# Three more modulation kinds summed by VectorE, inside the second chunks of three FFN stages

## The chip, the cores and the metric

One core of one Trainium2 chip runs the whole kernel. The metric is device time in microseconds (us), and the time of a kernel is the median of several runs. Three runs of the kernel before are shown here. All arithmetic is in 32-bit floats.

## The reference, cut to what matters

Two trunk layers are computed for 128 context tokens and 512 latent tokens, side by side (640 tokens, 1024 features). Every layer is FFN, token mixing, FFN, each behind a norm with shift and scale and each with a gate:

```python
mod = (silu(c) @ w_mod[l] + b_mod[l]).reshape(..., 3 * N_SUB, D_MODEL)   # 9 vectors a layer
modulated(j, y) = _rmsnorm(y, g[j]) * (1 + mod[:, :, 3*j+1]) + mod[:, :, 3*j]
x = x + 0.5 * mod[:, :, 2] * _swiglu(modulated(0, x), ffn_w_in[l, 0], ffn_w_out[l, 0])
_swiglu(h, w_in, w_out): g, u = split(h @ w_in); return (silu(g) * u) @ w_out
```

`c` is one vector for the latent tokens and `c_ctx` one for the context tokens. So each of the 18 modulation vectors ("kinds", 9 in each of 2 layers) is a product of two rows of 1024 numbers with a 1024 x 1024 block of `w_mod`.

## The kernel before, in words

**Stages.** FFN 0, the even mixer, FFN 1, FFN 2, the odd mixer, FFN 3; in the code `f` is the number of the FFN. The hidden width of 2816 is worked in 11 "doubles" `d` of 256 columns. Doubles 0 to 3, 4 to 7 and 8 to 10 form chunks 0, 1 and 2. After a chunk's doubles comes its output stretch of 8 units `u`, each 128 output features.

**A double.** From double 1 on, the two halves of the tokens and of the features are combined by a Strassen-like scheme with 7 products ("items" t = 0 to 6) in place of 8. Every product is made of three matmuls (high by high, high by low, low by high part), so an item is 2 column blocks x 4 k-tiles x 3 = 24 matmuls, and a double 168. For its items ScalarE rounds the raw weights to the high part (`item_hi`, L1907), VectorE subtracts to get the low part (`item_lo`, L2482), and VectorE forms four sums of raw weight quadrants in place (`weight_sum`, L2503). The low and high parts lie in a ring of 4 slots, so an item's split can run only when TensorE is done with the item 4 before.

**What stands in VectorE's queue.** `double(f, d)` of the vector block writes the order out by hand, and so do those of ScalarE and TensorE; each engine runs its own list in order. For a double that isn't the last of its chunk it is: `item_lo` 4 and 5, `add_p2` (L2795) of both column blocks s = 0, 1, `item_lo` 6, `item_lo` 0 of the next double, the two "c12" additions (L2832; block s waits for `u2_kept`, a copy by ScalarE at L2120), `weight_sum` 0 of the next double (it waits for both raw halves to have landed), "c22" of block 0 (L2842), the next `item_lo` 1, "c22" of block 1 (L2842), `weight_sum` 1, the next `item_lo` 2, `weight_sum` 2, four multiplications (L2860, L2862), `low_hidden` (L2781), the next `item_lo` 3, `low_hidden`, `weight_sum` 3. In the last double of a chunk the splits of the output weights (`out_lo`, L2488) take the place of those of the next double and there are no sums.

**What TensorE waits for.** Item 6 is added onto the bank that c22 reads, so the part of item 6 for block s waits for c22 of block s of the same double:

```python
def free_part(f, d, t, s):
    n = pairs_before(f, d) + s + 1
    ...
    elif t == 6:
        pe.wait_ge(c22_done, n)
```

**Modulation.** Kinds 0 and 1 come from an opening block. The other 16 are made in two ways while the FFNs run.
- By products: `w_mod` comes in 8 "grains" (one k-tile of all 1024 columns, 512 KB) for a kind, and TensorE multiplies them, 4 grains in a "window" that follows an item (`WINDOWS[f][d, t] = (kind, part)`, `mod_products`, L1200).
- By adding: VectorE runs 16 operations (8 grains x 2 vectors) `acc = grain * c + acc` (`add_grains`; L2575 for the first grain, L2578 for the others), then TensorE sums over the partitions (`acc_sums`, L1210). All 16 run between the updates of x in the output stretch of chunk 0 or 1, and `acc_sums` follows item 1 of the next double.

In both cases `keep_kind` (L2550 to L2557) then turns the result and stores it. Products use four grain buffers, adding uses two of them; the accumulators lie in the other two.

**SyncE** issues every load from one queue, in written order, and waits in it for a buffer to come free: `load_in` (w_in of the next double, raw half 0 after `item_lo` 4, raw half 1 after `item_lo` 6), `load_out`, `load_grain`.

Of the kernel before, what the change touches and what calls it, by code (L numbers as in the profile page):

```python
# [64 lines left out]
def trunk(nc, a, out):  # L65

    with ExitStack() as ctx:
# [753 lines left out]
        def _(sp):  # L821
# [62 lines left out]
            def ffn(f):  # L884

                for d in range(DOUBLES):
# [9 lines left out]
                    if last:  # L896
                        load_out(f, c, 0)
                        load_out(f, c, 1)
                    else:
                        load_in(f, d + 1, 0)  # L900
                        load_in(f, d + 1, 1)
# [2591 lines left out]
```

## Time and profile before

| | us |
|---|---|
| median of 3 runs | 2389.56 |
| lowest and highest run | 2386.39, 2391.74 |
| the profiled execution, its own time | 2391.84 |
| its span (first to last instruction) | 2390.1 |
| TensorE busy | 2339.1 |
| VectorE busy | 1581.4 |
| ScalarE busy | 956.8 |

The profile is of one execution. The span is what its views show; 1.74 us of that execution's time lie around it. Engines: PE is TensorE's matmuls, PEld its weight loads, DVE is VectorE, ACT ScalarE, SP SyncE. Two matmuls that follow each other overlap in the records (a matmul of 320 columns is shown as 0.31 us and the next begins 0.147 us after it), so durations of matmuls are not to be added; starts are to be compared.

### The profile page before, as it was taken

The page shows a single profiled execution, that of the slowest core. Times are in us where ns is not written, and L with a number is a line of the kernel's source. Part 1 is how long each engine was busy: PE and PEld are TensorE (multiplying, and loading weights), DVE is VectorE, ACT ScalarE, POOL GpSimd, SP SyncE. Part 2 cuts the span into 40 slices and gives each one's busy share as a digit, 9 for nine tenths or more (in the row PEclk, how much of TensorE's full clock was granted, in tenths as well). Part 3 has the DMA queues.
Part 4 walks back from the last instruction along what each step waited for, and adds up shares of the span by engine and source line. Part 5 has one row for each costly group of instructions (what it writes and reads, how often), then busy time and mean ns, then how long its engine had stood idle before and what let it go on. Part 6 is the DMA issues. An engine that isn't in the chain of part 4 may idle for free.

```text
span 2390.1 us, 39818 instructions
## 1 busy us (share of the span) xinstructions
PE 2339.1 (98%) x16652; PEld 2262.9 (95%) x16652; DVE 1581.4 (66%) x2414; ACT 956.8 (40%) x1497; POOL 0.2 (0%) x4
## 2 busy tenths in 40 slices
PE   7999999999989999999999999999999999999999
PEld 6999999999769999999999999999999999999998
DVE  5876676657767876777587767676245668467463
ACT  6533423344555423414364143244215255234242
POOL 0000000000000000000000000000000000000000
PEclk9999999999999999999999999999999999999999
DMA  8342545322101242434224344333221012322122
GB/s 293 124 157 94 191 141 176 128 67 71 39 19 54 89 159 92 139 124 142 89 79 170 106 159 159 106 111 99 88 71 45 19 54 71 106 71 89 58 93 71
DMA packets 201421, 251.62 MB, mean 105 GB/s; under 512 B 12994, under 2 KB 178074, under 8 KB 201242
## 3 DMA queue, kind: packets, MB, share of 16 engines
q1 hardware_dynamic: 201242, 249.07, 31.4%
q8 instruction: 132, 2.16, 0.4%
q14 instruction: 47, 0.39, 0.1%
HBM read 245.76 MB, written 3.28 MB: 104 GB/s over the span
## 4 chain that ended last, share of the span: by engine, by line
PE 84%; DVE 7%; issue 3%; ACT 3%; DMA 2%; SPq 0%; DVEq 0%; ACTq 0%
PE banks L1053 72%; DMA w_raw<-ffn_w_in 2%; DVE w_lo L2482 2%; PE banks L1200 1%; ACT w_hi L1907 1%; DVE w_raw L2503 1%; PE banks L1391 1%; PE banks L1393 1%; PE banks L1392 1%; PE banks L1478 1%; PE banks L1490 1%; ACT prob L2284 0%; DVE hid_lo L2781 0%; PE banks L1505 0%; PE banks L1671 0%
## 5 line engine op out<-in xcount | busy, mean ns | idle before, releaser
L1053 PE MATMUL banks<-b_hi,w_hi 128*128 128x320 f32 x2496 | 778.4, 312 | 14.3 <-DVE b_lo L2671 5.8
L1053 PE MATMUL banks<-b_hi,w_lo 128*128 128x320 f32 x2496 | 772.2, 309 | 0.0
L1053 PE MATMUL banks<-b_lo,w_hi 128*128 128x320 f32 x2496 | 772.1, 309 | 0.0
L1053 PEld LDWEIGHTS banks<-b_hi,w_hi 128*128 128x128 f32 x2496 | 469.4, 188 | 33.6 <-issue 23.4
L1907 ACT ACTIVATE w_hi<-w_raw 128x1024 fp32r<-128x1024 f32 x296 | 310.2, 1055 | 417.4 <-PE banks L1053 245.6
L2482 DVE TENSOR_TENSOR w_lo<-w_raw,w_hi 128x1024 fp32r<-128x1024 f32 x296 | 361.7, 1224 | 167.8 <-ACT w_hi L1907 166.1
L1053 PEld LDWEIGHTS banks<-b_lo,w_hi 128*128 128x128 f32 x2496 | 469.6, 188 | 0.0
L1053 PEld LDWEIGHTS banks<-b_hi,w_lo 128*128 128x128 f32 x2496 | 469.4, 188 | 0.0
L1053 PE MATMUL banks<-hid_hi,w_hi 128*128 128x320 f32 x1664 | 397.1, 311 | 3.0 <-DVE hid_lo L2781 1.5
L1053 PE MATMUL banks<-hid_hi,w_lo 128*128 128x320 f32 x1664 | 394.0, 309 | 0.0
L1053 PE MATMUL banks<-hid_lo,w_hi 128*128 128x320 f32 x1664 | 393.9, 309 | 0.0
L1053 PEld LDWEIGHTS banks<-hid_hi,w_hi 128*128 128x128 f32 x1664 | 281.7, 188 | 4.8 <-DVE hid_lo L2781 2.3
L1053 PEld LDWEIGHTS banks<-hid_lo,w_hi 128*128 128x128 f32 x1664 | 282.1, 188 | 0.0
L1053 PEld LDWEIGHTS banks<-hid_hi,w_lo 128*128 128x128 f32 x1664 | 281.9, 188 | 0.0
L2510 DVE SCALAR_TENSOR_TENSOR x<-banks,mod,x 128x128 f32<-128x128 f32 x354 | 135.0, 434 | 220.9 <-PE banks L1053 220.9
L2503 DVE TENSOR_TENSOR w_raw<-w_raw 128x1024 f32<-128x1024 f32 x160 | 195.4, 1221 | 17.1 <-DMA w_raw<-ffn_w_in 11.3
L1913 ACT ACTIVATE w_hi<-w_raw 128x1024 fp32r<-128x1024 f32 (+1 forms) x96 | 93.3, 984 | 236.4 <-PE banks L1053 236.4
L2091 ACT ACTIVATE hid_hi<-work 128x640 fp32r<-128x640 f32 x88 | 64.2, 734 | 159.7 <-DVE work L2862 149.0
L2488 DVE TENSOR_TENSOR w_lo<-w_raw,w_hi 128x1024 fp32r<-128x1024 f32 (+1 forms) x96 | 107.7, 1132 | 9.8 <-ACT w_hi L1913 9.1
L1896 ACT ACTIVATE w_hi<-w_raw 128x2048 fp32r<-128x2048 f32 (+1 forms) x26 | 48.0, 1847 | 103.4 <-PE banks L1053 49.4
L2832 DVE TENSOR_TENSOR work<-work,banks 128x320 f32<-128x320 f32 x80 | 38.0, 485 | 75.1 <-ACT work L2120 75.1
L2465 DVE TENSOR_TENSOR w_lo<-w_raw,w_hi 128x2048 fp32r<-128x2048 f32 (+1 forms) x24 | 52.8, 2202 | 47.1 <-ACT w_hi L1896 47.1
(330 smaller groups left out, 2549.5 us busy)
## 6 DMA issues: line engine op xcount, KB each, us to landing
w_raw<-ffn_w_in SPq DMA_DIRECT2D x176, 512.0 KB, 4.8
mod_grain<-w_mod SPq DMA_DIRECT2D x84, 512.0 KB, 6.0
w_raw<-ffn_w_out SPq DMA_DIRECT2D x64, 512.0 KB, 4.5
last_grain<-w_mod SPq DMA_DIRECT2D x44, 512.0 KB, 6.2
w_raw<-ffn_w_out SPq DMA_DIRECT2D x32, 384.0 KB, 3.7
w_raw<-w_in_odd SPq DMA_DIRECT2D x20, 512.0 KB, 4.7
mod_first<-w_mod SPq DMA_DIRECT2D x3, 2048.0 KB, 15.4
w_raw<-w_in_even SPq DMA_DIRECT2D x12, 512.0 KB, 4.9
```

Of the source, the lines that this page charges most:

```text
L1053: ins = pe.matmul(o, w3[w], v3[v][cols], start=first and i == 0, stop=last and i == 2, skip_group_check=onto_read)
L1200: ins = pe.matmul(bank[MODB][b * MOD_ROWS:(b + 1) * MOD_ROWS, 0:KIND_COLS], wide_c[:, kt, :], by_features(grain[q])[:, b], start=kt == 0, ...
L1896: act.activation(split_view(w_hi, kind, parity(unit)), raw_view(kind, parity(unit)), ACT.Copy).then_inc(hi_ready, 1)
L1907: act.activation(ring_in(w_hi, in_slot(d, t)), operand(d, t), ACT.Copy).then_inc(hi_ready, 1)
L1913: act.activation(ring_out(w_hi, out_slot(c, u), CHUNKS[c]), out_operand(c, u), ACT.Copy).then_inc(hi_ready, 1)
L2091: act.activation(hid_hi[:, k + s, :], work[:, s, 0:2, :].rearrange("p a b -> p (a b)"), ACT.Copy)\
L2465: dve.tensor_tensor(split_view(w_lo, kind, parity(unit)), raw_view(kind, parity(unit)), split_view(w_hi, kind, parity(unit)).bitcast(F32), ...
L2482: dve.tensor_tensor(ring_in(w_lo, q), operand(d, t), ring_in(w_hi, q).bitcast(F32), ALU.subtract).then_inc(lo_ready, 1)
L2488: dve.tensor_tensor(ring_out(w_lo, q, n), out_operand(c, u), ring_out(w_hi, q, n).bitcast(F32), ALU.subtract)\
L2503: dve.tensor_tensor(out_, in0, in1, op).then_inc(sums_done, 1)
L2510: ins = dve.scalar_tensor_tensor(out=xs, in0=bank[banks[hf]][:, in_bank], scalar=mod_col(v, layer, 3 * j + 2, d), in1=xs, op0=ALU.mult, op ...
L2832: dve.tensor_tensor(work[:, s, 1, :], work[:, s, 1, :], role(d, s, "C"), ALU.add).then_inc(c12_done, 1)
```

## The change

Before, six kinds are summed by adding (3, 6, 9, 11, 14, 16) and ten by products. After, nine are summed by adding (3, 4, 5, 9, 10, 11, 13, 14, 15) and seven by products (2, 6, 7, 8, 12, 16, 17). FFNs 0, 1 and 2 each keep two added kinds in the output stretches of chunks 0 and 1 and get a third (4, 10, 14), whose 16 operations are put inside doubles 4 to 7 (2, 4, 4 and 6 of them), at five slots of VectorE's list. Its `acc_sums` follows item 6 of double 7, its `keep_kind` the last `out_lo` of that double, and its grains are loaded between those of the weights. The windows move: FFN 0 loses the four of doubles 5 and 6; FFN 1 loses (5, 1) and (6, 1) and gets (2, 4) and (3, 4); FFN 2 loses (2, 1), (3, 1), (5, 1), (6, 1) and gets (9, 4) and (10, 4). The first two grains of an outer kind are now issued behind the first two loads of the output weights.

```diff
-        WINDOWS = ({(1, 4): (2, 0), (2, 4): (2, 1), (5, 1): (4, 0), (5, 4): (4, 1), (6, 1): (5, 0), (6, 4): (5, 1),
-                    (9, 1): (7, 0), (9, 4): (7, 1), (10, 1): (8, 0), (10, 4): (8, 1)},
-                   {(5, 1): (10, 0), (6, 1): (10, 1), (9, 1): (12, 0), (10, 1): (12, 1)},
-                   {(2, 1): (13, 0), (3, 1): (13, 1), (5, 1): (15, 0), (6, 1): (15, 1), (9, 1): (17, 0), (10, 1): (17, 1)}, {})
-        ADDED = ({0: 3, 1: 6}, {0: 9, 1: 11}, {0: 14, 1: 16}, {})
-        SUMS_AT = (4, 1), (8, 1)
+        WINDOWS = ({(1, 4): (2, 0), (2, 4): (2, 1), (9, 1): (6, 0), (9, 4): (6, 1), (10, 1): (7, 0), (10, 4): (7, 1)},
+                   {(2, 4): (8, 0), (3, 4): (8, 1), (9, 1): (12, 0), (10, 1): (12, 1)},
+                   {(9, 1): (16, 0), (9, 4): (16, 1), (10, 1): (17, 0), (10, 4): (17, 1)}, {})
+        ADDED_OUT = ({0: 3, 1: 5}, {0: 9, 1: 11}, {0: 13, 1: 15}, {})
+        ADDED_IN = ({1: 4}, {1: 10}, {1: 14}, {})
+        SUMS = [{**{(doubles_until(c), 1): kind for c, kind in ADDED_OUT[f].items()},
+                 **{(doubles_until(c) - 1, ITEMS - 1): kind for c, kind in ADDED_IN[f].items()}} for f in range(4)]
         ADD_OPS = (3, 3, 3, 3, 2, 1, 0, 1)
+        DOUBLE_OPS = {1: (2, 4, 4, 6)}
+        SLOT_OPS = {2: (0, 0, 0, 2, 0), 4: (0, 0, 1, 2, 1), 6: (1, 1, 1, 2, 1)}
         HALF_KIND = KT // 2
-        FIRST_WINDOW = ((1, 4), None, (2, 1), None)
+        FIRST_WINDOW = ((1, 4), (2, 4), None, None)
...
@@ SyncE, ffn(f), in double d
+                    inner, outer = ADDED_IN[f].get(c), ADDED_OUT[f].get(c) if last else None
+                    done = ops_before(f, d)
+                    ready = done + DOUBLE_OPS[c][d - CHUNK_PARTS * c] if inner is not None else None
+                    if last:
+                        load_out(f, c, 0)
+                    else:
+                        load_in(f, d + 1, 0)
+                    if inner is not None and done // 2 + 2 < (ready + 1) // 2:
+                        load_grain(inner, done // 2 + 2)
+                    if last:
+                        load_out(f, c, 1)
+                    else:
+                        load_in(f, d + 1, 1)
+                        if inner is not None:
+                            for kt in range(max(done // 2 + 2, (ready + 1) // 2), min(ready // 2 + 2, KT)):
+                                load_grain(inner, kt)
+                    if outer is not None:
                         if c == 0 and FIRST_WINDOW[f] is None:
                             rows_free(f)
-                        load_grain(added, 0)
-                        load_grain(added, 1)
...
@@ VectorE, double(f, d)
+                def add_slot(i):
+
+                    if c in ADDED_IN[f]:
+                        slots = SLOT_OPS[DOUBLE_OPS[c][d - CHUNK_PARTS * c]]
+                        add_grains(ADDED_IN[f][c], ops_before(f, d) + sum(slots[:i]), slots[i])
+
                 item_lo(f, d, 4)
+                add_slot(0)
                 if d == 1:
                     form_low(f, 5, quadrants(f)[2][:, :, :])
                 item_lo(f, d, 5)
+                add_slot(1)
                 if d == 1:
                     form_low(f, 6, quadrants(f)[1][:, :, :])
                 for s in range(2):
                     add_p2(f, d, s)
+                    if s == 0:
+                        add_slot(2)
                 item_lo(f, d, 6)
                 if not last and d > 1:
                     item_lo(f, d + 1, 0)
+                add_slot(3)
                 for s in range(2):
+                    if s == 1:
+                        add_slot(4)
                     dve.wait_ge(u2_kept, done + s + 1)
                     dve.tensor_tensor(work[:, s, 1, :], work[:, s, 1, :], role(d, s, "C"), ALU.add).then_inc(c12_done, 1)
...
-                if kind_done is not None:
+                if kind_done is not None and kind_done not in ADDED_IN[f].values():
                     keep_kind(kind_done)
...
                     out_lo(f, c, 3)
+                    if c in ADDED_IN[f]:
+                        keep_kind(kind_done)
```

## Rows read from the trace of the kernel before

**Rows 1.** The page: busy time of each engine.

```profile
PE 2339.1 (98%) x16652; PEld 2262.9 (95%) x16652; DVE 1581.4 (66%) x2414; ACT 956.8 (40%) x1497; POOL 0.2 (0%) x4
```

**Rows 2.** Windows: length; busy us (records) by engine; clock, DMA share, GB/s.

```profile
2130.91:2155.55 24.64, 24.64 (x170) 24.64 (x169) 18.76 (x24) 11.89 (x17) 0.00 (x0) 1.00 0.27 87
1392.77:1419.47 26.70, 26.70 (x202) 25.58 (x201) 19.98 (x30) 12.01 (x17) 0.00 (x0) 1.00 0.45 158
913.18:939.01 25.83, 25.83 (x186) 25.05 (x185) 15.50 (x19) 10.97 (x15) 0.00 (x0) 1.00 0.46 164
```

**Rows 3.** VectorE, FFN 3, double 5: start, length, what, idle before.

```profile
2142.77 1.23 DVE L2482 TENSOR_TENSOR w_lo<-w_raw,w_hi 128x1024 fp32r<-128x1024 f32 x1 [0.59 <-ACT w_hi L1907]
2146.35 1.23 DVE L2482 TENSOR_TENSOR w_lo<-w_raw,w_hi 128x1024 fp32r<-128x1024 f32 x1 [2.35 <-ACT w_hi L1907]
2147.49 0.48 DVE L2832 TENSOR_TENSOR work<-work,banks 128x320 f32<-128x320 f32 x1
2149.18 0.49 DVE L2832 TENSOR_TENSOR work<-work,banks 128x320 f32<-128x320 f32 x1 [1.21 <-ACT work L2120]
2149.59 1.22 DVE L2503 TENSOR_TENSOR w_raw<-w_raw 128x1024 f32<-128x1024 f32 x1
...
2153.07 0.48 DVE L2842 TENSOR_TENSOR work<-work,banks 128x320 f32<-128x320 f32 x1
```

**Rows 4.** FFN 3, double 6: VectorE and the matmul that waits.

```profile
2175.15 1.23 DVE L2503 TENSOR_TENSOR w_raw<-w_raw 128x1024 f32<-128x1024 f32 x1 [0.83 <-DMA w_raw<-ffn_w_in]
...
2178.64 0.48 DVE L2842 TENSOR_TENSOR work<-work,banks 128x320 f32<-128x320 f32 x1
...
2179.18 0.41 PE L1053 MATMUL banks<-b_hi,w_hi 128*128 128x320 f32 x1 [0.26 <-DVE work L2842]
```

**Rows 5.** Windows: FFN 3 doubles 6 and 9, FFN 1 double 5.

```profile
2155.55:2181.03 25.48, 25.14 (x170) 24.64 (x169) 18.76 (x24) 11.88 (x17) 0.00 (x0) 1.00 0.26 83
2286.63:2312.52 25.89, 25.14 (x170) 24.64 (x169) 18.77 (x24) 11.89 (x17) 0.00 (x0) 1.00 0.26 82
939.01:967.11 28.10, 27.21 (x203) 25.59 (x201) 19.98 (x30) 12.00 (x17) 0.00 (x0) 1.00 0.44 150
```

**Rows 6.** VectorE before weight_sum 0: FFN 3 double 9, FFN 1 double 5.

```profile
961.22 1.23 DVE L2503 TENSOR_TENSOR w_raw<-w_raw 128x1024 f32<-128x1024 f32 x1 [1.39 <-DMA w_raw<-ffn_w_in]
...
2306.63 1.23 DVE L2503 TENSOR_TENSOR w_raw<-w_raw 128x1024 f32<-128x1024 f32 x1 [1.24 <-DMA w_raw<-ffn_w_in]
```

**Rows 7.** VectorE, FFN 0, output stretch.

```profile
313.94 1.41 DVE L2575 TENSOR_SCALAR mod_grain<-mod_grain,wide_c 128x1024 f32<-128x1024 f32 x2
315.27 1.28 DVE L2578 SCALAR_TENSOR_TENSOR mod_grain<-last_grain,wide_c,mod_grain 128x1024 f32<-128x1024 f32 x1
316.46 1.13 DVE L2510 SCALAR_TENSOR_TENSOR x<-banks,mod,x 128x128 f32<-128x128 f32 x3
```

**Rows 8.** VectorE, FFN 0, double 4.

```profile
220.22 0.49 DVE L2832 TENSOR_TENSOR work<-work,banks 128x320 f32<-128x320 f32 x1 [1.22 <-ACT work L2120]
```

**Rows 9.** VectorE, FFN 3, double 7, the last of its chunk.

```profile
2188.75 1.23 DVE L2482 TENSOR_TENSOR w_lo<-w_raw,w_hi 128x1024 fp32r<-128x1024 f32 x1 [0.38 <-ACT w_hi L1907]
...
2199.30 0.49 DVE L2832 TENSOR_TENSOR work<-work,banks 128x320 f32<-128x320 f32 x1 [1.27 <-ACT work L2120]
2200.25 1.23 DVE L2488 TENSOR_TENSOR w_lo<-w_raw,w_hi 128x1024 fp32r<-128x1024 f32 x1 [0.46 <-ACT w_hi L1913]
2201.39 0.48 DVE L2842 TENSOR_TENSOR work<-work,banks 128x320 f32<-128x320 f32 x1
```

**Rows 10.** Grains into buffers 0 to 2, FFN 1's first output stretch.

```profile
DMA to landing us min/median/max: 3.4/3.4/6.9
```

**Rows 11.** Windows: double 2 of FFNs 1, 2 and 3.

```profile
803.99:832.22 28.23, 25.82 (x170) 24.63 (x169) 21.87 (x27) 13.55 (x19) 0.00 (x0) 1.00 0.35 113
1255.50:1283.92 28.42, 27.64 (x203) 25.57 (x201) 22.21 (x27) 13.66 (x19) 0.00 (x0) 1.00 0.54 197
1997.45:2025.31 27.86, 25.71 (x170) 24.64 (x169) 21.81 (x26) 13.57 (x19) 0.00 (x0) 1.00 0.26 77
```

More of the change, by code:

```diff
@@ L610, in trunk, with kinds_before, ops_before @@
         ffn_tables(3)
-        WINDOWS = ({(1, 4): (2, 0), (2, 4): (2, 1), (5, 1): (4, 0), (5, 4): (4, 1), (6, 1): (5, 0), (6, 4): (5, 1),
[3 rows of a table removed]
-        ADDED = ({0: 3, 1: 6}, {0: 9, 1: 11}, {0: 14, 1: 16}, {})
-        SUMS_AT = (4, 1), (8, 1)
+        WINDOWS = ({(1, 4): (2, 0), (2, 4): (2, 1), (9, 1): (6, 0), (9, 4): (6, 1), (10, 1): (7, 0), (10, 4): (7, 1)},
[5 more added lines that the diff above has]
+                 **{(doubles_until(c) - 1, ITEMS - 1): kind for c, kind in ADDED_IN[f].items()}} for f in range(4)]
         ADD_OPS = (3, 3, 3, 3, 2, 1, 0, 1)
+        DOUBLE_OPS = {1: (2, 4, 4, 6)}
+        SLOT_OPS = {2: (0, 0, 0, 2, 0), 4: (0, 0, 1, 2, 1), 6: (1, 1, 1, 2, 1)}
         HALF_KIND = KT // 2
-        FIRST_WINDOW = ((1, 4), None, (2, 1), None)
-        BY_ADDING = [kind for f in range(4) for kind in ADDED[f].values()]
-        BY_PRODUCTS = [kind for kind in range(FIRST_KIND, DEPTH * 3 * N_SUB) if kind not in BY_ADDING]
+        FIRST_WINDOW = ((1, 4), (2, 4), None, None)
+        KIND_ORDER = tuple(range(2, DEPTH * 3 * N_SUB))
+        BY_PRODUCTS = (2, 6, 7, 8, 12, 16, 17)
+        BY_ADDING = [kind for kind in KIND_ORDER if kind not in BY_PRODUCTS]
+        def kinds_before(kind):
+            return KIND_ORDER[:KIND_ORDER.index(kind)]
         def products_before(kind):
-            return KT * sum(k < kind for k in BY_PRODUCTS)
+            return KT * sum(k in BY_PRODUCTS for k in kinds_before(kind))
         def adds_before(kind):
-            return 2 * KT * sum(k < kind for k in BY_ADDING)
+            return 2 * KT * sum(k in BY_ADDING for k in kinds_before(kind))
         def added_before(kind):
-            return sum(k < kind for k in BY_ADDING)
+            return sum(k in BY_ADDING for k in kinds_before(kind))
+        def ops_before(f, d):
+            c = chunk_of(d)
+            return sum(DOUBLE_OPS[c][:d - CHUNK_PARTS * c]) if c in ADDED_IN[f] else 0
         def grain_buf(kind, kt):
@@ L642, in trunk @@
         buf_loads, buf_user = [0] * GRAIN_BUFS, [None] * GRAIN_BUFS
-        for kind in range(FIRST_KIND, DEPTH * 3 * N_SUB):
+        for kind in KIND_ORDER:
             for kt in range(KT):
@@ L660, in added_at @@
         def added_at(f, d, t):
-            return ADDED[f].get(SUMS_AT.index((d, t))) if (d, t) in SUMS_AT else None
+            return SUMS[f].get((d, t))
         def kind_done_at(f, d):
@@ L889, in ffn @@
                         load_window(f, where)
-                    added = ADDED[f].get(c) if last else None
-                    if added is not None:
+                    inner, outer = ADDED_IN[f].get(c), ADDED_OUT[f].get(c) if last else None
[15 more added lines that the diff above has]
+                    if outer is not None:
                         if c == 0 and FIRST_WINDOW[f] is None:
                             rows_free(f)
-                        load_grain(added, 0)
-                        load_grain(added, 1)
[L896 to L901, printed above, removed]
+                        load_grain(outer, 0)
+                        load_grain(outer, 1)
                     if last:
@@ L904, in ffn @@
                         load_out(f, c, 3)
-                    if added is not None:
+                    if outer is not None:
                         for kt in range(2, 5):
-                            load_grain(added, kt)
+                            load_grain(outer, kt)
                     if last and d + 1 < DOUBLES:
                         load_in(f, d + 1, 0)
-                    if added is not None:
+                    if outer is not None:
                         for kt in range(5, KT):
-                            load_grain(added, kt)
+                            load_grain(outer, kt)
                     if last and d + 1 < DOUBLES:
                         load_in(f, d + 1, 1)
+                        if c + 1 in ADDED_IN[f]:
+                            load_grain(ADDED_IN[f][c + 1], 0)
+                            load_grain(ADDED_IN[f][c + 1], 1)
                     if d + 1 < DOUBLES:
@@ L1181, in bank_free @@
             def bank_free(f, kind):
[L1183 removed]
+                if kind == KIND_ORDER[0]:
                     pe.wait_ge(first_prod, 2 * f + 2)
                 else:
[L1186 removed]
+                    pe.wait_ge(kind_kept, len(kinds_before(kind)))
             def by_features(tile):
@@ L2898, in ffn @@
                     tail = final and after[0] is not None
-                    added = ADDED[f].get(c)
+                    added = ADDED_OUT[f].get(c)
                     if added is not None:
```

2 lines of the change are left out of this document (removed).

## The prediction, on record before the changed kernel was run

> **What bounds the kernel now.** I read the page first. TensorE is busy for 2339.1 of 2390.1 us and VectorE for 1581.4, two thirds [rows 1]. The average makes VectorE look free, so the question is where in a double the free time lies. The view of windows gives the price of TensorE's own work: a double without modulation takes 24.64 us and has no idle time (busy 24.64), one with a window takes 26.70 us, one with an `acc_sums` 25.83 us [rows 2]. So a window costs 2.06 us, an `acc_sums` 1.19 us, and TensorE alone sets the pace there.
>
> Then I read VectorE's timeline of such a double [rows 3]. It is busy for 18.76 of 24.64 us. From the start of the double (2130.91 us), `item_lo` 6 runs at +11.86, then 2.35 us pass idle until the next `item_lo` 0 at +15.44, which waits for ScalarE, as that waits for a ring slot. The c12 additions follow at +16.58 and +18.27, with 1.21 us idle between them, since block 1 waits for ScalarE's copy. `weight_sum` 0 starts at +18.68 and c22 of block 1 at +22.16. Behind c12 nothing is idle but short waits on ScalarE for results of VectorE itself.
>
> c22 has hardly any room. In double 6 of FFN 3 `weight_sum` 0 waited 0.83 us for a weight load, c22 of block 1 ended at 2178.64 + 0.48 = 2179.12, and TensorE's next matmul, idle for 0.26 us, started at 2179.18 with "DVE work L2842" as what ended its wait [rows 4]. That double took 25.48 us, 0.84 more than 24.64. Two others took 25.89 against 24.64 and 28.10 against 26.70, so 1.25 and 1.40 us were lost [rows 5], and there the same wait was 1.24 and 1.39 us [rows 6]. A delay of `weight_sum` 0 is lost one for one. Exactly: it started at +18.68 in double 5 of FFN 3, at +19.60 in double 6 and at +20.00 in double 9, 0.92 and 1.32 us late for 0.84 and 1.25 us lost; the room is 0.08 us.
>
> **The change, part by part.**
>
> *TensorE's work.* Product kinds go from ten to seven, that is 20 to 14 windows: 6 x 2.06 = 12.36 us saved. `acc_sums` go from six to nine: 3 x 1.19 = 3.57 us added. Balance: -8.79 us.
>
> *The operations added to VectorE.* The first grain's take (315.27 - 313.94) / 2 = 0.67 us each, the others 316.46 - 315.27 = 1.19 us from start to start [rows 7]. 6 and 42 of them make 54 us in twelve doubles.
>
> *Double 4 (two short ones, slot 3).* They stand in front of c12: 1.33 us. The idle time between the two c12 additions is 1.22 us in this double too [rows 8], and is now used up, since ScalarE's copy for block 1 is ready by then. c12 of block 1 is late by about 0.03 to 0.11 us, within the room. Loss 0.
>
> *Doubles 5 and 6 (four each; slots 2, 3, 3, 4).* The one in slot 2 delays `item_lo` 6 by 0.6 us (1.19 less the 0.59 it waited) and with it the load of raw half 1; the 2.35 us idle behind it swallow the rest. Two stand in slot 3, behind the next `item_lo` 0, so the 2.35 us are no cover for them: c12 of block 0 starts at 2147.49 + 2.38 = 2149.87. Then 0.40 for it, and the slot 4 operation, 1.19, sits in front of c12 of block 1, which starts at 2151.46 instead of 2149.18 [rows 3]: 2.28 us late. `weight_sum` 0 and both c22 follow 2.28 us late, and TensorE loses 2.28 - 0.08 = 2.20 us. The weight load has more slack than before, so lateness of a load as in [rows 6] no longer adds. TensorE's stall moves the next double's start by the same amount, and `item_lo` 0 hangs on TensorE, so the delay starts anew in each double and doesn't pile up: 2 x 3 x 2.20 = 13.2 us. Bounds: 0, if idle time that I don't see covers them, and 3 x 1.19 = 3.57 us per double, if none does; 0 to 21.4 us in all. I take the worked value, as [rows 4 to 6] show this very path.
>
> On the price of one such operation the Trainium skill says, in VectorE: DVE Perf Modes, section Mode 1× (REGULAR) — the baseline, that an operation with two tensor inputs in 32 bits gives one result a cycle, and the page's clock is 0.96 GHz; that is an estimate of 1.07 us for 1024 elements, against 1.19 us in the row [rows 7]. By the page each of these doubles would lose 3 x 0.12 = 0.36 us less and the sum would be 2.2 us lower; the row is this very instruction, and the sum goes by it.
>
> *Double 7 (six; slots 1, 1, 1, 2, 1), the last of the chunk.* I walk FFN 3's double 7, with 1.14 us from start to start for a split and 0.40 for a small addition [rows 3, 9]. `item_lo` 4 at 2188.75; an operation, `item_lo` 5, an operation: to 2193.41; `add_p2`, operation, `add_p2`, `item_lo` 6, an operation: to 2197.73. The next one needs grain 7. Its load is issued only when the operation that ended at about 2193.5 is done, behind half of the output weights. Grains landed 3.4 to 6.9 us after issue, median 3.4 [rows 10]; with another load just ahead I take 4.5, so 2198.0. Then this operation, c12 of block 0, the last operation, and c12 of block 1 starts at 2200.8 instead of 2199.30, `out_lo` 0 at 2201.2 instead of 2200.25 (it waited 0.46 us on ScalarE before, so that part is covered), and c22 is 0.95 us late. c22 of block 0 ended at 2201.87 [rows 9] and TensorE was due at 2181.03 + 21.12 = 2202.15 (six of seven items); less 0.15 for the signal that is 0.13 of room: 0.8 us lost. With no wait for the grain it is 0.5, with 6.9 us it is 3.2. Three FFNs: 2.4 us, bounds 1.5 and 9.6, and 0 if c22 isn't what counts.
>
> *What is behind the chunk.* `keep_kind` (some 2 us) now stands behind `out_lo` 3 and ahead of the first x update. VectorE, some 5 us late there, has TensorE's next unit (7 us) before that update is asked for: 0. The outer kind's first grains are issued by the middle of double 7, over 10 us ahead of their use: 0. `acc_sums` behind item 6 finds its sums done.
>
> *Windows moved.* Double 2 of an FFN has stalls of its own: 28.23 us in FFN 1 and 27.86 in FFN 3 without a window, 28.42 in FFN 2 with one [rows 11]. So FFN 2's window there cost only 0.37 us, and taking it away gives 0.37 and not 2.06: +1.69. FFN 1 gets one behind item 4 of double 2, where it can hide those stalls that come later: between 0 and the 1.69 of FFN 2; I take -1.1. FFN 1's double 5 loses its window and the grain loads that delayed its weights, so the 1.40 us lost there go: -1.40 (its new stall is in the 13.2).
>
> **Sum.** -12.36 + 3.57 + 13.2 + 2.4 + 1.7 - 1.1 - 1.4 = +6.0 us on the profiled execution's 2391.84, or 2397.8. That execution is 2.28 above the median 2389.56; taken from the median: 2395.6 us.
>
> **Rivals.**
>
> *A. The operations fit into VectorE's idle time (faster).* The place is c12 to c22 in doubles 5 and 6. For it: the two waits of a double, 2.35 + 1.21 = 3.56 us, are just what three operations need (3.57). If what `item_lo` 0 waits for weren't tied to TensorE's pace, or if TensorE had more room at item 6 than 0.08 us, the whole 13.2 + 2.4 = 15.6 us of stalls would be gone: 6.0 - 15.6 = -9.6, so 2380.0. It decides from c22 of block 1 being done before +22.7. Against it: the order of the slots, and three doubles that lost what they were late. 10 in 100.
>
> *B. Grain 7 is late.* It lands 6 to 7 us after issue as the slowest in [rows 10]; double 7 then loses 2.3 to 3.2 and not 0.8: 4.5 to 7 us more, 2400 to 2402.5. For it: its load has no lead. Against: most single grains land in 3.4. 14 in 100.
>
> *C. The stalls are there but the small terms go the other way.* The stalls of FFN 2's double 2 don't return (1.7 less), and double 7 costs nothing (2.4 less): +1.9, 2391.5, no difference that can be measured. 19 in 100.
>
> **How the numbers follow.** The forecast has 57 in 100. What a measurement here can tell from no change is about 0.2%, 4.8 us, so slower means above 2394.3. My forecast is only 1.3 above that; with its own spread of some 2 us I give 43 of the 57 to slower and 14 to the same. Slower 43 + 14 (B) = 57, same 14 + 19 (C) = 33, faster 10 (A). The range 2388.5 to 2401.5 holds the forecast, C and most of B, and leaves out A and the far end of B.
>
> **What would show it.** Right: in the changed profile doubles 5 and 6 of FFNs 0, 1 and 2 take 26.8 us, with TensorE waiting for "DVE work L2842" (the line moves) by some 2 us; double 4 takes 25.83; double 7 takes 25.4 up to item 7 plus 1.19; c12 of block 0 starts 2.4 us behind the end of the next `item_lo` 0. FFN 0 is faster by some 2 us, FFNs 1 and 2 slower by 4 each. Wrong: doubles 5 and 6 at 24.64 (A); VectorE waiting over 2 us for `mod_grain` or `last_grain` in double 7 (B); a stall growing from double 5 to 6, or waits on `w_lo` in doubles 5 to 7, would show that the delays pile up, which I exclude.

## The result: slower by 13.7 us, the direction as forecast, the size more than twice as large

The changed kernel takes 2403.24 us, the median of five runs (2402.27 to 2405.49). The kernel before takes 2389.56, five runs too (2386.39 to 2391.74). The ratio is 1.0058, with a 95% interval of 1.0047 to 1.0069. The forecast was +6.0 us, 2395.6, with a range up to 2401.5; the measured +13.7 lies beyond that range. The profiled executions differ by 2403.24 - 2391.84 = 11.4 us and their spans by 11.3, which is what the traces can account for. The 2.3 us that are left are the distance of the profiled run of before from its own median.

The page after, its first line and the line of `items`' matmuls (columns as in [rows 1]; behind the bar busy time, mean ns, idle time just before and what ended most of it):

```profile
PE 2334.1 (97%) x16508; PEld 2260.9 (94%) x16508; DVE 1633.4 (68%) x2462; ACT 956.6 (40%) x1497; POOL 0.2 (0%) x4
...
L1078 PE MATMUL banks<-b_hi,w_hi 128*128 128x320 f32 x2496 | 779.6, 312 | 30.6 <-DVE work L2880 18.2
```

Against [rows 1] VectorE has 52 us more to do, close to the 54 of the forecast. TensorE is busy 5.0 us less, and these matmuls now wait 18.2 us for c22 (L2842 before is L2880 now); in the same group of the kernel before it was 2.7.

The windows of doubles 4 to 7 of FFNs 0, 1 and 2 in the changed kernel, four rows for each FFN, answer to [rows 2, 5] (length; busy us of PE, PEld, DVE, ACT and POOL with their numbers of records; granted clock, DMA share, GB/s):

```profile
200.70:226.53 25.83, 25.83 (x186) 25.05 (x185) 16.71 (x21) 10.97 (x15) 0.00 (x0) 1.00 0.36 117
226.53:254.63 28.10, 25.15 (x170) 24.65 (x169) 24.43 (x34) 11.89 (x17) 0.00 (x0) 1.00 0.37 113
254.63:281.78 27.15, 25.14 (x170) 24.64 (x169) 23.36 (x28) 11.88 (x17) 0.00 (x0) 1.00 0.38 116
281.78:308.12 26.34, 25.97 (x187) 24.96 (x185) 24.24 (x32) 11.68 (x17) 0.00 (x0) 1.00 0.48 158
916.33:942.17 25.84, 25.84 (x187) 25.06 (x186) 16.72 (x21) 10.96 (x15) 0.00 (x0) 1.00 0.37 119
942.17:971.42 29.25, 26.22 (x171) 25.99 (x169) 25.15 (x35) 11.77 (x17) 0.00 (x0) 0.94 0.35 109
971.42:998.26 26.84, 25.14 (x171) 24.64 (x169) 22.71 (x27) 12.00 (x17) 0.00 (x0) 1.00 0.39 118
998.26:1025.43 27.17, 25.98 (x187) 24.97 (x185) 24.24 (x32) 11.67 (x17) 0.00 (x0) 1.00 0.50 161
1371.62:1397.45 25.83, 25.83 (x186) 25.05 (x185) 16.71 (x21) 10.97 (x15) 0.00 (x0) 1.00 0.37 117
1397.45:1425.45 28.00, 25.14 (x171) 24.65 (x169) 24.43 (x34) 11.88 (x17) 0.00 (x0) 1.00 0.37 113
1425.45:1454.65 29.20, 26.51 (x170) 26.05 (x169) 24.35 (x29) 11.77 (x17) 0.00 (x0) 0.94 0.35 108
1454.65:1480.39 25.74, 25.74 (x187) 24.96 (x185) 23.32 (x31) 11.67 (x17) 0.00 (x0) 1.00 0.47 155
```

Double 4 loses nothing (25.83). FFN 0 is 0.5 us faster than before from double 1 to double 10, FFNs 1 and 2 are 6.5 and 6.7 us slower, where the forecast had 2 faster and 4 slower each. FFN 1's double 6 is 26.84 - 24.64 = 2.20 us above the plain double, exactly the stall worked out. The other five are not: doubles 5 have 3.46, 4.61 and 3.36 us, doubles 6 of FFNs 0 and 2 have 2.51 and 4.56. The six stalls come to 20.7 us and not 13.2. These 7.5 us are what the prediction lacks, and the experiments are about them. Two of the rows have a granted clock of 0.94, where all those of [rows 2, 5] have 1.00.

*Where double 5 loses more.* VectorE's timeline in the changed kernel, FFN 0, from the end of double 4 (start, length, what, idle time before; double 5 starts at 226.53):

```profile
229.68 0.31 DVE L2575 STREAM_TRANSPOSE mod_turn<-banks 128x128 f32<-128x128 f32 x1
...
231.36 0.83 DVE L2806 TENSOR_TENSOR hid_lo<-work,hid_hi 128x640 fp32r<-128x640 f32 x1 [0.21 <-ACT hid_hi L2116]
...
235.57 1.23 DVE L2507 TENSOR_TENSOR w_lo<-w_raw,w_hi 128x1024 fp32r<-128x1024 f32 x1 [0.38 <-ACT w_hi L1932]
...
243.22 1.22 DVE L2507 TENSOR_TENSOR w_lo<-w_raw,w_hi 128x1024 fp32r<-128x1024 f32 x1 [1.71 <-ACT w_hi L1932]
244.37 1.28 DVE L2603 SCALAR_TENSOR_TENSOR mod_grain<-last_grain,wide_c,mod_grain 128x1024 f32<-128x1024 f32 x1
...
246.76 0.48 DVE L2870 TENSOR_TENSOR work<-work,banks 128x320 f32<-128x320 f32 x1
```

The outer kind's `keep_kind` (six small operations, 229.68 to 231.14) stands ahead of `low_hidden`, so `item_lo` 4 starts at 235.57, +9.04. In the kernel before, in double 5 of FFN 3, which starts at 2130.91, it is at +7.65:

```profile
2138.56 1.23 DVE L2482 TENSOR_TENSOR w_lo<-w_raw,w_hi 128x1024 fp32r<-128x1024 f32 x1 [0.38 <-ACT w_hi L1907]
```

The next `item_lo` 0 starts at +16.69 and not at +15.44, that is 1.25 us late. From there on all is as forecast: c12 of block 0 (246.76) starts 2.39 us behind the place right after `item_lo` 0 (244.37), where the first of the two operations now stands. ScalarE's timeline names the link between the two:

```profile
242.13 1.06 ACT L1932 ACTIVATE w_hi<-w_raw 128x1024 fp32r<-128x1024 f32 x1 [3.77 <-DMA w_raw<-ffn_w_in]
```

ScalarE waits for raw half 0, which is loaded once `item_lo` 4 has freed it: that operation ends at 236.80, SyncE issues the load at 236.82, and it has landed at 242.12. Late operation, late issue, late landing.

### The profile page after: what moved, and what is told of

The parts are those of the page before. It is cut to its first block, busy times and chain, and to the rows that moved or that the text cites. A ratio compares the mean times of both kernels' runs of the same rounds, so it can differ in the third digit from the quotient of the medians.

```text
span 2401.4 us, 39602 instructions
## 1 busy us (share of the span) xinstructions
PE 2334.1 (97%) x16508; PEld 2260.9 (94%) x16508; DVE 1633.4 (68%) x2462; ACT 956.6 (40%) x1497; POOL 0.2 (0%) x4
## 4 chain that ended last, share of the span: by engine, by line
PE 79%; DVE 10%; issue 4%; ACT 4%; DMA 3%; SPq 0%; DVEq 0%; ACTq 0%
PE banks L1078 67%; DMA w_raw<-ffn_w_in 2%; DVE w_lo L2507 2%; ACT w_hi L1932 2%; DVE w_raw L2528 1%; DVE mod_grain L2603 1%; PE banks L1225 1%; PE banks L1416 1%; PE banks L1418 1%; PE banks L1417 1%; PE banks L1503 1%; PE banks L1515 1%; DVE hid_lo L2806 1%; ACT prob L2309 0%; PE banks L1530 0%
## 5 line engine op out<-in xcount | busy, mean ns | idle before, releaser
L1078 PE MATMUL banks<-b_hi,w_hi 128*128 128x320 f32 x2496 | 779.6, 312 | 30.6 <-DVE work L2880 18.2
L2603 DVE SCALAR_TENSOR_TENSOR mod_grain<-last_grain,wide_c,mod_grain 128x1024 f32<-128x1024 f32 x72 | 91.1, 1279 | 0.9 <-DMA last_grain<-w_mod 0.9
```

Source lines behind the costliest of these rows:

```text
L1078: ins = pe.matmul(o, w3[w], v3[v][cols], start=first and i == 0, stop=last and i == 2, skip_group_check=onto_read)
L2603: ins = dve.scalar_tensor_tensor(out=acc, in0=grain[q], scalar=c_of, in1=acc, op0=ALU.mult, op1=ALU.add)
```

## The experiments

Eleven kernels ran, in three groups, each group with its own runs of the kernel before: medians 2391.13 (24 runs), 2390.26 (18) and 2390.25 (17). Ratios are to these.

**e1_order.** The changed kernel with slot 3 ahead of the next `item_lo` 0.

```diff
+                add_slot(3)
                 if not last and d > 1:
                     item_lo(f, d + 1, 0)
-                add_slot(3)
```

> Theory P (place): TensorE's loss in doubles 5 and 6 comes from the two operations that stand behind the next item_lo 0, in front of c12 and c22. Here they stand ahead of it, in the 2.35 us that VectorE waits there; everything else is as in the changed kernel. P: double 6 loses 0.3 to 0.4 us instead of 2.2 to 4.6, double 5 about 1.1 (its weight load of half 0 is late) instead of 3.4 to 4.6, TensorE's clock doesn't fall, and the kernel takes 2385 to 2390 us instead of 2403.2. Rival L (load): what counts is how much work VectorE has in a double, and the order of two neighbours is indifferent: 2402 to 2404, doubles 5 and 6 as before.

Measured: 2392.23 us (11 runs), ratio 1.0004 [0.9995, 1.0013], 11 us below the changed kernel. The stalls of doubles 5 fell to 1.7, 2.2 and 1.7 us and those of doubles 6 to 0.4, 0.5 and 1.1. So the place of two operations behind `item_lo` 0 is worth most of the stall, as the prediction's timeline had it: the 2.35 us of idle time ahead of `item_lo` 0 [rows 3] are a cover only for what stands ahead of it. It missed the expected 2385 to 2390 by some 2 us, in doubles 5. Against the kernel before it is no difference that can be measured.

**e2_short.** The operations of the inner kinds on 8 of 1024 columns (this leaves most of these kinds' sums out), loads and waits as they are.

```diff
+                    n_cols = 8 if kind in (4, 10, 14) else GRAIN
-                    acc, c_of = mod_acc[:, v, :], wide_c[:, kt, v:v + 1]
+                    acc, c_of = mod_acc[:, v, 0:n_cols], wide_c[:, kt, v:v + 1]
```

> Leaves out: the 16 operations inside doubles 4 to 7 work on 8 of 1024 columns, so kinds 4, 10 and 14 are not summed. Number, order, signals and DMAs are those of the changed kernel. Both P and L: the operations' length is gone (some 0.1 us each), doubles 5 and 6 lose at most 0.5 us each, double 7 nothing, and what is left is the change in TensorE's own work and in the early doubles: 2379 to 2382 us. Rival G (grains): the loads of the grains between those of the weights, or the number of instructions and signals, make the weights late; then doubles 5 and 6 still lose over 1 us each and the kernel takes over 2388.

Measured: 2383.75 us (8 runs), ratio 0.997 [0.996, 0.998], 1.75 us above the expected range. Double 7 costs 1.09 us in all three FFNs, nothing beyond its `acc_sums`, so grains and their loads have no price of their own there. But doubles 5 still lose 0.6, 0.9 and 0.7 us and doubles 6 of FFNs 0 and 2 lose 0.5 and 1.0, with almost no work added. The time of the operations is not the cause of that.

**e4_both.** All the work, spread 5, 3, 3, 5, slot 3 ahead as in e1_order, and the outer kind kept at the opening of double 4.

```diff
-        DOUBLE_OPS = {1: (2, 4, 4, 6)}
-        SLOT_OPS = {2: (0, 0, 0, 2, 0), 4: (0, 0, 1, 2, 1), 6: (1, 1, 1, 2, 1)}
+        DOUBLE_OPS = {1: (5, 3, 3, 5)}
+        SLOT_OPS = {0: (0, 2, 0, 2, 1), 1: (0, 0, 0, 2, 1), 2: (0, 0, 0, 2, 1), 3: (1, 1, 1, 1, 1)}
```

> All 48 operations are there, but each stands where VectorE waits: 5, 3, 3, 5 of them in doubles 4 to 7, always two ahead of the next item_lo 0 and one between the two c12; acc_sums of the outer kind follows item 0 and its keep_kind opens doubles 4 and 8, so that double 5 doesn't start late. P: no double of the three second chunks loses more than 0.5 us but for a late weight load (up to 1.3 us, one or two of them), and the kernel takes 2379 to 2384 us, faster than both. L: VectorE has the same work, so 2400 or more.

Measured: 2387.56 us (11 runs), ratio 0.9983 [0.9974, 0.9992]. Faster than both kernels, and some 4 us above what was expected. Doubles 5 lose 0.4, 0.2 and 0, but doubles 4 lose 1.2, 0.5 and 0.3 and doubles 6 of FFNs 0 and 2 1.9 and 1.5. In the three that lose over 1 us a weight load lands late.

**e5_probe.** The kernel before with scratch operations in FFN 3, which feed nothing. It ran once, as did e7_probe, and both are read by the lengths of FFN 3's doubles alone.

```diff
+                ahead, behind, between = PROBES.get((f, d), (0, 0, 0))
                 item_lo(f, d, 6)
+                probe(ahead)
                 if not last and d > 1:
                     item_lo(f, d + 1, 0)
+                probe(behind)
                 for s in range(2):
+                    if s == 1:
+                        probe(between)
                     dve.wait_ge(u2_kept, done + s + 1)
```

> The kernel before with operations added in FFN 3 alone, which has no modulation (a scratch result of the same form, 128 x 1024, 1.19 us each; 9 of them). Double 5: two behind the next item_lo 0 and one between the c12, as in the change. Double 6: two ahead of the next item_lo 0 and one between. Double 9: three behind and one between. P: double 5 takes 24.64 + 2.20 = 26.8 us, double 6 24.7 to 25.0 (24.64, the small excess, and up to 0.8 if its load is late), double 9 28.1 (four times 1.19, less 1.21 and 0.08 = 3.47), and if a stall of 3.4 us lowers TensorE's clock, up to 1.7 more. L: doubles 5 and 6 lose the same.

Windows of FFN 3's doubles 5 and 9 in e5_probe:

```profile
2130.97:2157.81 26.84, 25.13 (x171) 24.64 (x169) 22.17 (x27) 11.88 (x17) 0.00 (x0) 1.00 0.25 80
2288.05:2317.33 29.28, 26.53 (x170) 26.04 (x169) 24.39 (x29) 11.88 (x17) 0.00 (x0) 0.94 0.23 72
```

Two behind `item_lo` 0 and one between cost 26.84 - 24.64 = 2.20 us to the hundredth; two ahead and one between cost nothing (double 6: 24.64). Three behind and one between cost 29.28 - 24.64 = 4.64, where one operation more than in double 5 gives 2.20 + 1.19 = 3.39 (the 3.47 of the expectation is 0.08 too much). The row has the reason, a clock of 0.94.

**e3_keep.** The changed kernel with `acc_sums` of the outer kind one item earlier and its `keep_kind` at the opening of doubles 4 and 8. Nothing else moves.

```diff
-        SUMS = [{**{(doubles_until(c), 1): kind for c, kind in ADDED_OUT[f].items()},
+        SUMS = [{**{(doubles_until(c), 0): kind for c, kind in ADDED_OUT[f].items()},
...
+                outer_done = SUMS[f].get((d, 0))
+                if outer_done is not None:
+                    keep_kind(outer_done)
                 item_lo(f, d, 4)
```

> The changed kernel with all its operations in their slots (2, 4, 4, 6), and one thing moved: the outer kind's acc_sums stands one item earlier and its keep_kind opens doubles 4 and 8 instead of closing them. Theory K (keep_kind at the end of double 4 delays item_lo 4 of double 5 by 1.4 us, and by it the load of raw half 0 and the next item_lo 0): the stall of double 5 falls from 3.45, 4.61 and 3.35 us in FFNs 0, 1, 2 to the 2.20 that the prediction had, the granted clock no longer falls in FFN 1's double 5, double 6 keeps its 2.2 to 2.5, and the median is 3.5 to 4.5 us below the changed kernel's 2403.2: 2399 to 2400. Rival J (the load of half 0 is late by the lateness of transfers alone): double 5 keeps 3.3 us or more in at least two FFNs, 2402 to 2404. Rival S (the keep_kind's 1.4 us is only moved): double 4 loses what double 5 gains, 2402 to 2404.

Measured: 2400.51 us (5 runs), ratio 1.0036 [1.0023, 1.0048]. Windows of doubles 5 and 6 of FFNs 0, 1, 2:

```profile
226.22:253.06 26.84, 25.14 (x171) 24.64 (x169) 23.30 (x28) 11.88 (x17) 0.00 (x0) 1.00 0.38 118
253.06:280.89 27.83, 25.13 (x170) 24.63 (x169) 23.36 (x28) 11.77 (x17) 0.00 (x0) 1.00 0.37 114
...
941.31:968.15 26.84, 25.14 (x171) 24.64 (x169) 23.30 (x28) 11.88 (x17) 0.00 (x0) 1.00 0.38 119
968.15:994.99 26.84, 25.14 (x170) 24.64 (x169) 23.36 (x28) 11.88 (x17) 0.00 (x0) 1.00 0.38 118
...
1393.85:1420.70 26.85, 25.14 (x170) 24.65 (x169) 23.32 (x28) 11.88 (x17) 0.00 (x0) 1.00 0.38 118
1420.70:1449.20 28.50, 25.14 (x171) 24.64 (x169) 23.36 (x28) 11.76 (x17) 0.00 (x0) 1.00 0.36 111
```

All three doubles 5 lose exactly 2.20 us now, and double 4 nothing: theory K holds in its mechanism and in the size of the stall. The median is 2.7 us below the changed kernel's and not 3.5 to 4.5, because doubles 6 of FFNs 0 and 2 came to 3.2 and 3.9 us.

**e6_order_keep.** e1_order and e3_keep together.

> Both of the moves together, operations 2, 4, 4, 6: slot 3 stands ahead of the next item_lo 0 (as in e1_order) and keep_kind opens double 4 (as in e3_keep). If the two causes are separate (place of slot 3; late start of double 5), the gains add: e1_order's 2392.2 falls by 1.2 to 1.5 us for each of three doubles 5 (its stalls there of 1.7, 2.2 and 1.7 us become 0.4 to 0.6), 2387.5 to 2389. If the order alone had hidden the late start already, it stays at 2392. TensorE's granted clock stays at full in all FFN doubles.

Measured: 2387.26 us (11 runs), ratio 0.9983 [0.9974, 0.9992]. The gains add: doubles 5 lose 0.4, 0.7 and 0.8 us. Doubles 6 keep 0.5, 0.7 and 1.6.

**e8_split.** The same with another split.

```diff
+        DOUBLE_OPS = {1: (4, 3, 3, 6)}
+        SLOT_OPS = {0: (0, 1, 0, 2, 1), 1: (0, 0, 0, 2, 1), 2: (0, 0, 0, 2, 1), 3: (1, 1, 1, 2, 1)}
```

> Both moves and another split, 4, 3, 3, 6 operations in doubles 4 to 7, so that doubles 5 and 6 hold just the three that the two waits (2.35 + 1.21 us) cover, two ahead of the next item_lo 0 and one between the c12 additions. Theory P: doubles 5 and 6 lose 0 to 0.4 us each except where a transfer is late, double 4 loses 0 to 0.5, double 7 0.5 to 1.5; total of stalls about 5 us against 20.7 + 2 in the changed kernel: 2385 to 2387.5. Rival L (transfers that become later as VectorE's work moves toward its loads): as e4_both, one or two doubles of each FFN lose 1.5 us more, 2387.5 to 2389.

Measured: 2386.05 us (8 runs, 2382.64 to 2389.86), ratio 0.9981 [0.997, 0.9992]. Doubles 4 lose nothing, doubles 5 nothing, doubles 6 0.2, 0 and 0.7. It is 4 us faster than the kernel before. Its runs overlap with those of e4_both, e6_order_keep and e11_split_fetch, so that it is the best of the four is not shown.

**e7_probe.** e5_probe's operations placed anew.

```diff
-            PROBES, probes = {(3, 5): (0, 2, 1), (3, 6): (2, 0, 1), (3, 9): (0, 3, 1)}, [0]
+            PROBES, probes = {(3, 5): (0, 3, 1), (3, 6): (0, 2, 1), (3, 9): (0, 2, 1)}, [0]
```

> The kernel before with scratch multiply-adds in FFN 3 alone (on x, into the free sums' buffer; their results are used by nothing). Double 5: three behind the next item_lo 0 and one between the c12 additions, so a stall of 3.39 us if the delay is lost one for one; double 6: two behind and one between, 2.20 us; double 9: the same two and one, where the kernel before lost 1.25 us to a late load. Theory C (a stall of about 3 us or more of TensorE is followed by a stretch at the lower granted clock, and one of 2.2 is not): double 5 takes 24.64 + 3.39 + 0.8 to 1.1 = 28.8 to 29.1 us with a granted clock of 0.5 for 3.4 us behind the stall; double 6 takes 26.84 at full clock. Rival: the clock falls by chance, not by the stall: double 5 takes 28.03 at full clock. Double 9: 26.84 if the late load and the operations hide one another (the longer counts), 28.1 if they add.

Windows of FFN 3's doubles 5, 6 and 9, and of the stretch behind double 5's stall:

```profile
2132.49:2161.51 29.02, 26.38 (x170) 26.15 (x169) 24.25 (x29) 11.88 (x17) 0.00 (x0) 0.94 0.24 74
2161.51:2188.35 26.84, 25.14 (x170) 24.64 (x169) 21.46 (x26) 11.99 (x17) 0.00 (x0) 1.00 0.26 79
2293.95:2320.79 26.84, 25.14 (x170) 24.64 (x169) 22.18 (x27) 11.88 (x17) 0.00 (x0) 1.00 0.26 79
2153.00:2161.00 8.00, 5.36 (x27) 5.13 (x26) 7.17 (x10) 3.26 (x4) 0.00 (x0) 0.79 0.01 2
```

Double 5 lost 29.02 - 24.64 = 4.38 us: 3.39 by the operations and 1.0 by the clock. Double 9 lost 2.20 and not 2.20 + 1.25, but it doesn't test what it was built for: its half 1 landed at +18.59 and not at +19.91 as in the kernel before, so no load was late. Double 6 tests it. Its half 1 landed at +19.57 (+19.50 in the kernel before, where it cost 0.84 us), `weight_sum` 0 started at +20.96 behind the operations without waiting for it, and the double lost 2.20. So a late half 1 and operations on VectorE hide one another, and the longer counts.

**What makes half 0 late in double 6.** In the queues of FFN 2's double 6, from the issue of half 0 (1434.4) to its landing (1441.0), the changed kernel has one packet that FFN 1's double 6 (979.4 to 984.8) has not. The queues in FFN 2 (queue and kind: packets, MB, share of 16 engines):

```profile
q1 hardware_dynamic: 1195, 1.19, 58.2%
q8 instruction: 1, 0.02, 0.9%
```

In FFN 1 the view has the first line alone (1056 packets). The two transfers of half 0 from issue to landing, FFN 2 and then FFN 1:

```profile
DMA to landing us min/median/max: 4.4/5.3/6.2
...
DMA to landing us min/median/max: 3.9/4.4/4.9
```

These packets are 16 KB each. The changed kernel has 131 of them, one for 256 of its 33,544 recorded instructions on TensorE (matmuls, weight loads and their sequencer's), some 18.4 us apart; that they carry TensorE's program is inferred from this count. Over the changed kernel and nine of its variants there are 80 loads of half 0 in doubles 5 and 6. In 17 such a packet starts between the issue of the first transfer and a microsecond before the landing of the second, and the second takes 5.2 to 6.9 us. In the other 63 it takes 4.7 to 5.1. The two groups don't overlap. In FFN 2's double 6 a packet lay there in all ten kernels, so for this double there is no load without one to compare.

**e9_fetch.** The changed kernel with the same satisfied wait repeated on TensorE near the start, which shifts where the packets fall.

```diff
-            pe.wait_ge(rows_in, 16 * 7)
+            for _ in range(58):
+                pe.wait_ge(rows_in, 16 * 7)
```

> The changed kernel with 58 waits more on TensorE near the start (the same wait on rows_in, long satisfied, in front of the transposes of small_rows, where TensorE has idle time soon behind). Nothing else is changed. The traces so far show one DMA packet of kind 'instruction' (16 KB, queue 8) for about every 256 instructions of TensorE, some 18.4 us apart. Theory F (such a packet, when it falls between a weight load's issue and its landing, makes the load land 0.4 to 2 us later): the packets move about 4 us earlier, so that of FFN 2's double 6 (at +12.25 us, half 0 landed at +15.6 instead of +14.2) and of FFN 0's (at +9.55, landed at +14.6) leave the load's stretch; double 6 of FFN 2 loses 2.2 us instead of 4.6, FFN 0's 2.2 instead of 2.5, and double 7 of FFN 1 (packet at +10.8, landed at +16.2) 0.5 instead of 1.4; nothing in doubles 5: 3.6 us less, 2399 to 2400.5. Rival (lateness is of the address or by chance): the landings of half 0 in FFN 2's double 6 stay at +15.6 to +16.1 as in all six kernels with the change's windows so far, 2402.5 to 2404.

The trace shows 29 instructions more on TensorE and not 58, and the packets of the two doubles moved by 2.1 and 2.4 us and not by 4: in FFN 0's double 6 from +9.55 to +7.43 and in FFN 2's from +12.25 to +9.84. FFN 0's left its load's stretch, half 0 landed at +14.1 and the double lost 2.20. FFN 2's stayed in it, nearer its start; half 0 landed at +14.7 instead of +15.6 and the double lost 2.6 instead of 4.6, 1.1 of which is the clock, which stayed at full here. The median is 2401.59 (2398.39 to 2404.92, 5 runs), above the expected 2399 to 2400.5, and its runs overlap with those of the changed kernel: at this length of kernel the median doesn't tell it, the traces do.

**e10_keep_fetch.** e3_keep and e9_fetch together, every operation in the changed kernel's slots.

> e3_keep (keep_kind opens double 4) and the 58 waits of e9_fetch. If the three causes (start of double 5, instruction packets beside the loads, clock) are all that the prediction lacked, every one of the six doubles 5 and 6 loses the 2.20 us that it worked out, where no packet falls into a half 0 load, and the median is what it forecast, 2395 to 2397 (e3_keep: 2400.5, less 1.0 for FFN 0's double 6, 1.7 for FFN 2's, 0.9 for FFN 1's double 7). If something else holds the doubles, 2399 to 2401.

Measured: 2396.03 us (7 runs, 2395.04 to 2397.5), ratio 1.0026 [1.0015, 1.0036]. Windows of the six doubles 5 and 6:

```profile
226.30:253.17 26.87, 25.13 (x171) 24.64 (x170) 23.30 (x28) 11.88 (x17) 0.00 (x0) 1.00 0.39 118
253.17:280.00 26.83, 25.13 (x170) 24.63 (x169) 23.36 (x28) 11.88 (x17) 0.00 (x0) 1.00 0.38 118
...
939.89:966.73 26.84, 25.13 (x170) 24.64 (x169) 23.30 (x28) 11.88 (x17) 0.00 (x0) 1.00 0.38 119
966.73:993.58 26.85, 25.15 (x171) 24.65 (x170) 23.37 (x28) 11.88 (x17) 0.00 (x0) 1.00 0.38 118
...
1392.31:1419.15 26.84, 25.13 (x170) 24.64 (x169) 23.30 (x28) 11.88 (x17) 0.00 (x0) 1.00 0.39 118
1419.15:1446.30 27.15, 25.13 (x171) 24.64 (x169) 23.36 (x28) 11.88 (x17) 0.00 (x0) 1.00 0.37 116
```

The stalls are 2.23, 2.19, 2.20, 2.21, 2.20 and 2.51, in sum 13.5 us where the prediction had 13.2. The 2.51 has a packet beside its half 0 still (+9.41). The median is 5.8 us above its own kernel before, where the forecast had 6.0. So with `keep_kind` out of the way and the packets mostly clear of half 0's loads, the term of doubles 5 and 6 comes out as worked. That the whole time does so too is in part luck: the profiled executions' spans differ by 3.9 us alone, and terms that the sum left out (below) lower it.

**e11_split_fetch.** e8_split with e9_fetch's waits.

> e8_split and the 58 waits of e9_fetch. Its loads have more slack: doubles 6 of FFNs 0 and 2 lost only 0.2 and 0.6 us, double 7 of FFN 1 1.6 instead of 0.6. Theory F: 1 to 2 us less than e8_split's 2386.05, 2384 to 2385.5. Rival (packets fall elsewhere beside other loads and cost as much there): 2386.

Measured: 2385.93 us (11 runs), ratio 0.9982 [0.9973, 0.9991], so no gain over e8_split. FFN 0's double 6 loses 0.2 us as before, its packet gone from the load's stretch, but doubles 5 of FFNs 0 and 2 lose 0.8 and 1.2 us and double 6 of FFN 1 1.8, and in all three a packet now lies beside half 1. FFN 2's double 6 loses 1.4: a packet lies beside its half 0, and its half 1 takes 6.6 us with none beside it, which stays unexplained. The rival holds: a shift moves this price about and doesn't remove it.

## Why the prediction was right in direction and wrong in size

*What held.* Six windows less gave 2.06 us each, -12.36 in all. The three `acc_sums` more cost some 1.1 us each behind item 6 of double 7 (25.74 - 24.64 in FFN 2, and the same in e2_short), for 1.19; the 0.1 is counted below with double 7. Double 4 lost nothing. The mechanism of doubles 5 and 6 (two operations behind the next `item_lo` 0, one between the c12 additions, 0.08 us of room) gave 2.20 us to the hundredth wherever nothing else came in: FFN 1's double 6, e5_probe, e7_probe, e3_keep. FFN 2's double 2 got its stalls back: it became shorter by 0.35 us and not by 2.06, +1.71 for +1.7. FFN 1's window hid 1.54 us for my 1.1, and its double 5 is no longer held by half 1.

*The step that failed* is the term of doubles 5 and 6, 13.2 us, which came out as 20.7. Two sentences carry it. "The weight load has more slack than before, so lateness of a load as in [rows 6] no longer adds": this is true of half 1, which `weight_sum` 0 waits for (e7_probe's double 6), and false of half 0, which has to be there before ScalarE's split for `item_lo` 0. In double 5 of FFN 3 in the kernel before, half 0 lands at +13.99 and that split starts at +14.34, so it has about 0.3 us to spare, and everything behind `item_lo` 0 hangs on it. And "the delay starts anew in each double" was worked out from double 5 of FFN 3, which has no `keep_kind` ahead of it. I read [rows 8] for double 4's c12 and didn't follow its tail into double 5. The 7.5 us are:

- 1.25 + 1.59 + 1.15 = 4.0 us in doubles 5, by the late start. The same late `item_lo` 4 was in the kernel before (+9.02 in FFN 2's double 5), but there the double's window put the next `item_lo` 0 2.06 us later (+17.50), and nothing was lost. So taking the windows out gave 2.06 us each and uncovered this. Shown by e3_keep.
- 0.3 us in FFN 0's double 6 and 1.25 in FFN 2's, by half 0's late landing, with an instruction packet beside its load. The 80 loads show that the two go together, and e9_fetch and e10_keep_fetch have them move together: in FFN 0's double the packet left and the 0.3 us went, in FFN 2's it only came to lie nearer the start, and 0.4 and 0.3 us stayed.
- 0.83 us in FFN 1's double 5 and 1.12 in FFN 2's double 6, by TensorE's clock at a stall. Where the clock stayed at full, a double lost 0.76 or 0.77 us more than its pause (3.46 for 2.69 us, 3.36 for 2.59, and e3_keep's 3.86 for 3.09); here it lost 1.58 (4.61 for 3.03) and 1.87 (4.56 for 2.69). Windows of the changed kernel, one inside each of the two stretches:

```profile
966.50:969.00 2.50, 2.50 (x9) 2.50 (x10) 1.94 (x3) 2.50 (x4) 0.00 (x0) 0.50 0.31 126
1451.00:1454.00 3.00, 3.00 (x13) 2.77 (x12) 2.90 (x4) 1.18 (x2) 0.00 (x0) 0.50 0.00 0
```

The clock is half there, and 3.00 us hold 13 matmuls where full speed, one every 0.147 us, has 20.

The prediction named a stall that grows from double 5 to 6 as a sign of delays that pile up. In FFN 2 it did grow, from 3.36 to 4.56 us. The parts above account for it without any piling up, and in e10_keep_fetch two stalls of 2.20 us follow each other in FFN 1 and don't grow.

*Small terms.* Double 7 took 26.34, 27.17 and 25.74 us, that is 0.51, 1.34 and -0.09 against 24.64 + 1.19, in sum 1.8 us for 2.4. In FFN 1 VectorE did wait 0.7 us for the last grain, with an instruction packet beside its load; that is rival B in small. Not in the forecast at all were -1.4 us: FFN 3's doubles 6 and 9 no longer lose 0.65 and 1.25 us, since their half 1 lands at +18.5 and +18.3 and not at +19.5 and +19.9, with the packets (at +16.26 and +13.74 in the kernel before) now at +18.24 and +17.73; the stretches between the FFNs and FFN 3's double 2 differ by +1.10, -1.65 and +1.04. The sum is -12.4 + 3.6 + 20.7 + 1.8 + 1.7 - 1.5 - 1.4 - 1.4 = +11.1 us, for 11.3 between the spans.

*The rivals.* A (the operations fit into idle time) is false as the change stands, and its condition is just what e1_order and e8_split bring about by putting two of them ahead of `item_lo` 0. By that alone (e1_order) the time is the kernel before's; with `keep_kind` moved too (e6_order_keep, e8_split) it falls below. C (small terms the other way) did not come: the stalls of FFN 2's double 2 returned, and double 7 cost 1.8 us. The range ended at 2401.5 because it held rival B and no late load, on a sum with exact 2.20s. The prediction's own upper bound for the six doubles, 21.4 us in place of 13.2, makes the sum 6.0 + 8.2 = +14.2 us, or 2403.8, and would have held the time; the range did not reach to it.

## What to carry to other kernels

Work that is taken off the critical engine may have been the cover of something else that is late. So before a window is counted as a full gain, follow the chain (load, split, first use) through the double without it, and begin at the tail of the double ahead, not in a clean one. A place in the order is worth more than an amount: three operations cost 2.20 us or nothing, by whether two of them stand behind or ahead of one instruction that waits on another engine. Where the transfers' slack is 0.3 us, give the sum an upper bound with each such load late once.

## What the runs showed of the hardware that I had not expected

The second 512 KB transfer of a weight half, with 4.9 us from issue to landing, took up to 6.9 when one 16 KB packet of instructions fell beside it. It does not always: in e7_probe's double 9 of FFN 3 a packet at +13.75 lay beside half 1, and the transfer took 5.1 us, where the kernel before with a packet at +13.74 has 6.4. Nor is it the only cause: half 1, which in FFNs 0 to 2 can have loads of grains beside it, took 6.3 and 7.0 us in doubles 4 and 6 of FFN 0 in e4_both with no packet there. The late loads of [rows 4 to 6] in the kernel before have one each: in FFN 3 packets at +16.26 and +13.74 lay beside their half 1, and in FFN 1's double 5 one at +15.00, just ahead of half 1's issue at +15.17 and with loads of grains beside it as well. The kernel before's queues between 2169 and 2175 us, where raw half 1 of [rows 4] is loaded:

```profile
q1 hardware_dynamic: 1086, 1.07, 56.3%
q8 instruction: 1, 0.02, 0.9%
```

With 29 instructions more in TensorE's stream near the start (e9_fetch) all of the 131 packets came earlier.

TensorE's granted clock fell from full (2.4 GHz) to 0.5 (1.2 GHz) for 3.4 us at some stalls and not at others. It fell after idle times of 2.64 (e7_probe), 2.69 and 3.03 (changed kernel) and 2.75 us (e5_probe), about one microsecond lost each time. It stayed at full after 2.58, 2.61 and 2.87 (e9_fetch), 2.59 and 2.69 (changed kernel, FFNs 2 and 0) and 3.09 us (e3_keep). The 2.20 us stalls (pauses of 1.44 us) never cost it, but in the odd mixer it fell at a pause of 1.87 us (kernel before, at 1877.28 us). So the length of the pause alone doesn't decide, and what does stays open. The Trainium skill says in TensorE: Matmul & The Clock Gate, section Part 1: The HAM clock gate, that the clock has two levels of this kind and that activity releases the lower one. The windows agree with both levels (1.00 and 0.50), and in each of these doubles the clock came back while TensorE was at work.
